# A layer of 16384 one-neuron experts, from gathered rows to one dense pass over the tables

## What is computed

```python
def block_fn(hb):                       # 128 tokens, width 1024
    t = hb.shape[0]
    q = (hb @ w_query).reshape(t, PEER_HEADS, 2, PEER_HALF)      # 8 heads, 2 halves of 128
    s = jnp.einsum('thpc,hpnc->thpn', q, sub_keys)               # 128 sub-keys a half
    v1, i1 = lax.top_k(s[:, :, 0], PEER_TOPK)                    # 16 each
    v2, i2 = lax.top_k(s[:, :, 1], PEER_TOPK)
    cand = (v1[..., :, None] + v2[..., None, :]).reshape(t, PEER_HEADS, PEER_TOPK * PEER_TOPK)
    cand_idx = (i1[..., :, None] * PEER_NKEYS + i2[..., None, :]).reshape(...)
    best, pos = lax.top_k(cand, PEER_TOPK)
    experts = jnp.take_along_axis(cand_idx, pos, axis=-1)        # of 16384
    gate = jax.nn.softmax(best, axis=-1)
    u = expert_u[experts]                                        # rows of 1024
    vsel = expert_v[experts]
    act = jax.nn.gelu(jnp.einsum('thkd,td->thk', u, hb), approximate=False)
    return jnp.einsum('thk,thkd->td', gate * act, vsel)
```

## Time and profile before

| | |
|---|---|
| timed runs | 1367.41, 1369.69 and 1555.32 us |
| median | 1369.69 us |
| profiled execution, first to last instruction (its own time) | 1367.2 us |
| PE / DVE / ACT / POOL busy | 1162.8 / 713.7 / 392.0 / 286.6 us |
| moved by DMA | 446.79 MB, 327 GB/s over the span |
| indirect DMA alone | 268.45 MB |
| first and last gather issued | 269.16 and 919.93 us |
| last matmul on gathered rows ends | 941.2 us |

### The profile page before, as it was taken

The page is one execution under the profiler, slowest core; times in us unless marked ns, Lnnn a source line. Parts: engine busy times, 40 slices in busy tenths (PEclk is TensorE's granted clock), DMA queues, the critical chain, the costliest instruction groups (busy, mean ns, idle before and its releaser), DMA issues.

```text
span 1367.2 us, 16345 instructions
## 1 busy us (share of the span) xinstructions
PE 1162.8 (85%) x5986; PEld 716.0 (52%) x5986; DVE 713.7 (52%) x1850; ACT 392.0 (29%) x1094; POOL 286.6 (21%) x275
## 2 busy tenths in 40 slices
PE   6999998989999987778777777778999998867896
PEld 4887877874555532223222223325978875332342
DVE  2365532487677777767777666644752515311112
ACT  2203532223333333333233334222531423000011
POOL 0000000024444444444444434440030000000000
PEclk9999999999999999999999999999999998999999
DMA  9711237399999999999999999997521474999996
GB/s 392 302 62 62 93 116 315 147 406 395 421 421 421 422 420 421 422 421 399 422 422 422 421 419 399 421 422 313 196 94 63 185 292 177 427 424 424 425 388 257
DMA packets 60283, 446.79 MB, mean 327 GB/s; under 512 B 6704, under 2 KB 7088, under 8 KB 10160
## 3 DMA queue, kind: packets, MB, share of 16 engines
q0 software_dynamic: 36864, 268.45, 47.5%
q1 hardware_dynamic: 22912, 175.97, 31.8%
q10 hardware_dynamic: 432, 1.40, 0.3%
HBM read 444.74 MB, written 1.05 MB: 326 GB/s over the span
## 4 chain that ended last, share of the span: by engine, by line
PE 52%; DMA 34%; DVE 6%; ACT 4%; issue 2%; SPq 0%; POOL 0%; DVEq 0%; ACTq 0%
DMA arena<-uv_in,arena 26%; PE bank L2478 12%; PE bank L2344 9%; DMA wring<-moe_in 4%; PE bank L2575 4%; PE bank L2821 3%; PE bank L2441 3%; PE bank L2837 2%; DMA wring<-stream_in 2%; DVE arena L1809 2%; PE bank L2780 2%; DMA arena<-moe_in 2%; PE bank L2572 2%; PE bank L2807 2%; PE bank L637 1%
## 5 line engine op out<-in xcount | busy, mean ns | idle before, releaser
L2478 PE MATMUL bank<-arena 128*128 128x512 f32 x1024 | 474.1, 606 | 116.9 <-ACT arena L1069 116.9
L1809 DVE CUSTOM_DVE_ANT_0 arena<-arena 128x1024 f32<-128x1024 f32 x256 | 314.0, 1226 | 192.5 <-DMA arena<-uv_in,arena 191.5
L787 POOL DMA_INDIRECT arena<-uv_in,arena x256 | 272.0, 1063 | 650.1 <-PE bank L2478 365.7
L2478 PEld LDWEIGHTS bank<-arena 128*128 128x128 f32 x1024 | 186.6, 191 | 374.3 <-ACT arena L1069 192.7
L1061 ACT ACTIVATE arena<-arena 128x2 f32<-128x2 f32 x128 | 26.2, 205 | 410.0 <-DVE arena L1809 409.8
L2344 PE MATMUL bank<-wring,arena 128*128 128x256 f32 x608 | 134.1, 381 | 1.0 <-DVE arena L1384 1.0
L2344 PEld LDWEIGHTS bank<-wring,arena 128*128 128x128 f32 x608 | 115.2, 191 | 17.7 <-DVE arena L1384 1.1
L1069 ACT ACTIVATE arena<-const,arena 128x128 f32<-128x128 f32 x256 | 86.7, 385 | 0.0
L2441 PEld LDWEIGHTS bank<-arena,wring 128*128 128x128 f32 x384 | 57.0, 196 | 20.2 <-issue 15.3
L2821 PE MATMUL bank<-arena 128*32 128x512 f32 x288 | 59.7, 616 | 7.5 <-DMA arena<-moe_in 4.9
L2821 PE MATMUL bank<-wring,arena 128*32 128x512 f32 x288 | 59.7, 620 | 7.2 <-DMA wring<-moe_in 7.2
(11 more groups left out here) (458 smaller groups left out, 1318.5 us busy)
## 6 DMA issues: line engine op xcount, KB each, us to landing
wring<-stream_in SPq DMA_DIRECT2D x67, 1024.0 KB, 8.9
wring<-moe_in SPq DMA_DIRECT2D x14, 2048.0 KB, 17.9
arena<-moe_in SPq DMA_DIRECT2D x26, 1024.0 KB, 17.7
arena<-moe_in SPq DMA_DIRECT2D x12, 2048.0 KB, 18.7
wring<-moe_in SPq DMA_DIRECT2D x13, 1024.0 KB, 14.2
arena<-uv_in,arena POOLq DMA_INDIRECT x256, 12.8
arena<-moe_in SPq DMA_DIRECT2D x4, 512.0 KB, 10.7
wring<-moe_in SPq DMA_DIRECT2D x4, 512.0 KB, 11.2
```

Of the source, the lines that this page charges most:

```text
L787: pool.indirect_dma_start(G[:, j, :], None, uv_d, src).then_inc(gathered[j], 16)
L1809: v.tensor_tensor_reduce(out=junk, in0=G[:, j, 0:D], in1=h2[:, t, :], scale=1.0, scalar=0.0, op0=ALU.mult, op1=ALU.add, accum_out=dots[:, ...
L2478: ins = mm(bank[1 + 2 * tile + c][:, :], diag[:, j, :], G[:, j, D + c * 512:D + (c + 1) * 512], start=False, stop=False, skip_group_check= ...
```

## The change

The gathers, dots and diagonals go. The whole layer is done for all 16384 experts and all 256 tokens:

- The ring and the arena become one tensor `big`, in which `G` is now 128 x 256 floats a partition: G[j, i, t] belongs to the expert i * 128 + j and token t. A block i is 128 experts with the same first key.
- **u pass** (PE L2575 in the changed kernel). SP brings u in pairs of blocks, `u_in(m)`: four transfers, each of 256 columns of the pair's 256 rows to 32 partitions. DVE transposes each block in squares of 32 (`turn_u`, L1737) into one of two buffers `UT`; PE multiplies with `h2P`, h2 with its features in the matching order (made by `spread_h2`), 8 matmuls of 256 tokens a block; ACT writes the GELU of a pair into G. Between the blocks DVE does the selection, 3 pieces a block up to block 35, then 2; PE the remaining 12 queries, one every third block; POOL the lookup of the chosen keys (seven instructions a unit), which was `decode` on DVE.
- **Weights** (PE L2586). The sum over a token's slots of gate times the two one-hot key vectors is a 128 x 128 matrix. For each token one matmul forms it: `hot2` is the one-hot of the second key (POOL subtracts, ACT takes Abs and then Relu of 1 - x), `hot1` the one-hot of the first times the gate (DVE, L1854). They go in 64 batches of four tokens. DVE multiplies G with them (`weigh`, L1861), in place.
- **v pass** (PE L2595). SP brings v in pairs of blocks, `v_in(c)`, five buffers, in which three stand where the raw u was; PE accumulates all eight groups of 128 features of all tokens in four banks. The last four pairs are done tile by tile. SP loads the second block's first eight chunks in between.
- Ahead of the layer `project_out(1)` comes before the first query, the modulation group 5 is loaded after the output projection's chunks instead of before, and the query chunks have places of their own.

```diff
+            def u_in(m):
+
+                i = block_of(2 * m)
+                for a in range(4):
+                    sp.dma_start(raw[m % 3][32 * a:32 * a + 32],
+                                 uv_d[i * P:(i + 2) * P, a * T:(a + 1) * T].rearrange("(g r) c -> r g c", r=32))\
+                      .then_inc(uv_here[RAW_HOME[m % 3]], 16)
+
+            def v_in(c):
+
+                sp.dma_start(vbuf[c % V_RING], uv_d[2 * c * P:(2 * c + 2) * P, D:].rearrange("(b j) d -> j b d", b=2))\
+                  .then_inc(uv_here[c % V_RING], 16)
...
+            sp.wait_ge(rms_sum, 4)
+            u_in(2)
+            for m in range(3, PAIRS_U):
+                sp.wait_ge(ut_ready, 2 * (m - 3) + 2)
+                u_in(m)
+            for c, last in ((1, 61), (4, 62), (0, 63)):
+                sp.wait_ge(ut_ready, 2 * last + 2)
+                v_in(c)
+            sp.wait_ge(uv_used, BLOCKS_U)
+            v_in(2)
+            v_in(3)
+            for c in range(V_RING, PAIRS_U):
+                sp.wait_ge(uv_used, BLOCKS_U + c + 1 - V_RING)
+                v_in(c)
...
         def _(pool):
-                pool.indirect_dma_start(G[:, j, :], None, uv_d, src).then_inc(gathered[j], 16)
...
+            for b in range(N_BATCH):
+                if b >= 4:
+                    pool.wait_ge(w_built, b - 3)
+                nc.gpsimd.tensor_tensor(hot2[b % 4], bc(lane, 1, BATCH), bc(key2T[:, BATCH * b:BATCH * (b + 1)], 2, P),
+                                        ALU.subtract).then_inc(hot2_ready, 1)
...
+                act.wait_ge(uv_used, 2 * m + 2)
+                nc.scalar.activation(G[:, i:i + 2, :].rearrange("p i t -> p (i t)"), bank[1 + m % 2][:, :], ACT.Gelu)\
+                  .then_inc(u_out, 1)
...
+            def turn_u(n):
+
+                m, b = n // 2, n % 2
+                dve.wait_ge(uv_here[RAW_HOME[m % 3]], u_landed(m))
+                if n >= 2:
+                    dve.wait_ge(uv_used, n - 1)
+                v.transpose(UT[b].rearrange("p c (g r) -> p g c r", g=4),
+                            raw[m % 3][:, 4 * b:4 * b + 4, :].rearrange("p g (c s) -> p g c s", c=8)).then_inc(ut_ready, 1)
...
+            pieces = selection()
+            for n in range(BLOCKS_U):
+                if n >= 2:
+                    turn_u(n)
+                advance(pieces, 3 if n < PIECES_FAST else 2)
+                if n in GATES_AT:
+                    gates_of(GATES_AT.index(n))
...
+                for q in range(BATCH):
+                    tok = slice(BATCH * b + q, BATCH * b + q + 1)
+                    ins = v.tensor_scalar(hot1[:, b % 2, q], lane, key1T[:, tok], gateT[:, tok], ALU.is_equal, ALU.mult)
+                ins.then_inc(hot1_ready, 1)
+
+            def weigh(b):
+
+                dve.wait_ge(w_built, b + 1)
+                some = G[:, :, BATCH * b:BATCH * (b + 1)]
+                v.tensor_tensor(some, some, bank[W_BANK[b % 4]][:, :].rearrange("p (t i) -> p i t", t=BATCH), ALU.mult)\
+                 .then_inc(bank_taken, 1)
+
+            keys_hot(0)
+            keys_hot(1)
+            dve.wait_ge(u_out, PAIRS_U)
+            for b in range(N_BATCH):
+                weigh(b)
+                if b + 2 < N_BATCH:
+                    keys_hot(b + 2)
...
-            def weighted_rows(first, slots=range(GS)):
...
+                pe.wait_ge(ut_ready, n + 1)
+                for c in range(KD):
+                    ins = mm(bank[1 + m % 2][:, b * T:(b + 1) * T], UT[b][:, c, :], h2P[:, c, :],
+                             start=c == 0, stop=c == KD - 1)
+                ins.then_inc(uv_used, 1)
...
+            pe.wait_ge(u_out, PAIRS_U)
+            for b in range(N_BATCH):
+                pe.wait_ge(hot1_ready, b + 1)
+                pe.wait_ge(hot2_done, b + 1)
+                if b >= 4:
+                    pe.wait_ge(bank_taken, b - 3)
+                for q in range(BATCH):
+                    ins = mm(bank[W_BANK[b % 4]][:, q * P:(q + 1) * P], hot2[b % 4][:, q], hot1[:, b % 2, q],
+                             start=True, stop=True)
+                ins.then_inc(w_built, 1)
...
+            pe.wait_ge(bank_taken, N_BATCH)
+            for c in range(PAIRS_U - V_TAIL):
+                pe.wait_ge(uv_here[c % V_RING], v_landed(c))
+                for b in range(2):
+                    ins = values(c, b, range(KD), slice(0, T))
+                ins.then_inc(uv_used, 1)
```

More of the change, by code:

```diff
@@ L55, with chunk_slot, chunk_turn @@
 WSLOTS = 8
+RING = WSLOTS * CHUNK
+EXTRA_SLOTS = {C_Q: 8, C_SK: 9}
+def chunk_slot(n):
+    if C_Q <= n < C_IN2:
+        return EXTRA_SLOTS[n] if n in EXTRA_SLOTS else n - C_SK - 1
+    return n % WSLOTS
+def chunk_turn(n):
+    return sum(chunk_slot(m) == chunk_slot(n) for m in range(n + 1))
 SM = {}
@@ L81 @@
 CN_FIRST = CN["eps"].stop
-ARENA = 28928
+ARENA = 29400
 PER = 4
@@ new lines, in _ @@
+            for b in range(N_BATCH + 1):
+                if b < N_BATCH:
+                    act.wait_ge(hot2_ready, b + 1)
+                    steps[0] += 1
+                    nc.scalar.activation(hot2[b % 4], hot2[b % 4], ACT.Abs).then_inc(act_step, 1)
+                if b > 0:
+                    act.wait_ge(act_step, steps[0] - (b < N_BATCH))
+                    nc.scalar.activation(hot2[(b - 1) % 4], hot2[(b - 1) % 4], ACT.Relu, bias=ones[:, 0:1], scale=-1.0)\
+                      .then_inc(hot2_done, 1)
@@ new lines, in advance @@
+            def advance(pieces, n):
+                for _ in itertools.islice(pieces, n):
+                    pass
+            add_mixed(0)
+            finish_all(normed(0))
+            add_mixed(1)
+            turn_u(0)
+            turn_u(1)
+            finish_all(normed(1))
+            modulation(5)
+            pieces = selection()
[5 more added lines that the diff above has]
+                    gates_of(GATES_AT.index(n))
```

732 lines of the change are left out of this document (340 added, 392 removed).

## The result

The changed kernel takes 1800.57 us (median of four runs, 1797.19 to 1802.0), against 1369.69 us for the kernel before (median of 1367.41, 1369.69 and 1370.96): a ratio of 1.315, with a 95% interval of 1.3128 to 1.3177. It is slower by 31.5%. One run of before at 1555.32 us belongs to a slower state of the chip and is left out. The profiled execution took 1802.0 us, its span 1800.2.

A forecast was written before the change was run, and what follows sets the result against it. DMA's u stream at 210 GB/s was to bound most of the u pass: u's end at 600, weights 107, v 226.5 and what follows 423.5 gave a 1357 us span, median 1359, range 1318 to 1402.

The forecast's parts named there:

- The step that failed: u pass on PE: 8 matmuls of 128x256 a block at 0.216 us, 1.73 us a block, 221 us in all.
- 3.84 us for two: Before the u pass: price of two queries on PE, so four early queries were put at 8 us.
- The bound named for u: u pass: DMA's u stream at 210 GB/s, 2.49 us a block, above DVE's 2.2 and PE's 1.73.
- the three candidates: u pass: PE at 1.73 us a block, DVE at 2.7 then 2.2, DMA between 1.25 and 5.
- The stream at half the rate: u pass: four transfers to 32 partitions each move 210 GB/s, 4.97 us a pair of blocks.
- stream hidden: Rival for the u pass: four transfers together fill all DMA engines; 1328 us, chance 0.28 (hidden or nearly).
- The weights: Stage between u and v: 64 batches at 1.65 us with DVE the longest, 107 us.
- for some 30%: Weights: PE's busy share; its lower clock hidden there (0.5 us becomes 1), 3 us added at v's start.
- strided product: Rival for the weights: DVE's product on G takes double, 44 us more, 1403; weights dearer had 0.12.
- what follows the layer: After the v pass: 2.5 us off the 426.0 us of before, 423.5.
- the slow stream at 1659: u stream's lower end, a quarter of the rate: u pass 610 us, kernel 1659; at most 2 in 100.
- the prediction's own sign of error: u pass: the prediction called itself wrong if this pass is longer than 340 us.

The follow-up runs named there:

- the third experiment: Changed kernel with POOL making the differences of only the first four weights batches, ACT reusing those buffers for the other 60: 1761.28 us.
- the last: Kernel with u turned in HBM and one-instruction matmuls, with ACT making hot2 alone and POOL's subtraction gone: 1249.77 us, 0.9125 against before.

## Why the prediction was wrong

**The step that failed** is "a block is 8 matmuls of 128x256, and 272 of that form ran in 58.71 us, 0.216 each, so 1.73 us a block and 221 us in all", and with it the v pass, "960 matmuls of 128x256 at 0.216". The 0.216 is right. But the rows of the trace count instructions, the 8 and the 960 were counted in the code, and a float32 matmul of the code is two instructions. What stood ahead of the prediction shows it already: the order of the code lists a projection (L2414) with 64 matmuls and a query (L2441) with 16, and the earlier trace rows show the same two as x128 and x32. A group of before says it too. The code makes two matmuls of 512 columns for each of 256 pairs, 512:

```profile
L2478 PE MATMUL bank<-arena 128*128 128x512 f32 x1024 | 474.1, 606 | 116.9 <-ACT arena L1069 116.9
```

With 3.46 us a block, u is 128 x 3.46 + 12 queries with scores x 4.0 = 491, the 491.2 measured; v is (960 x 0.216 + 128 x 0.113) x 2 = 443.6, against 444.8. Both corrections, 181 and 218, are 399 of the 443 us by which the span was missed. The same error is in the queries ("3.84 us for two" is one query of 16 matmuls) and in the weights' four matmuls, which are eight instructions. The two projections, carried over as whole rows of 14.46 us, did not have it. That the u pass still began within 5 us of the forecast is partly luck: the four early queries took 15 us, not 8, and the projections ended at 265, not 259.5; against that the two spreadings took 4 us, not 7, and 290 held 8.5 us more than the terms listed for it.

The Trainium skill, "FP8 and Floating Point Precision", section "TensorE Precision Notes", says that true FP32 takes four passes through the array. The runs agree: 3.8 times between the two forms, in two instructions. The rule was not weighed in the prediction; it would not have changed the sum by itself, since 0.216 us for 256 columns holds two of the passes, and looks like one slow matmul as long as the counts are not compared.

**The bound named for u** was the wrong one of the three candidates, and rightly described. The stream at half the rate, taken as 210 GB/s, is 218 to 223 wherever it is the limit. Here the Trainium skill's figure for 32 partitions in "SBUF — State Buffer", section "Door 1: The DMA port swizzle", 218, was closer. Its statement in the section "Can I just issue two DMAs to hit both halves?" that transfers side by side hardly help each other also agrees. Neither is proved here, since no run moved pieces of 1 KB to 128 partitions. In the changed kernel the stream is hidden: 152 GB/s are wanted. So the rival "stream hidden" has its outcome but not its mechanism: four transfers together moved 219 GB/s where PE was out of the way, not 421, and PE was slow enough to hide even half the rate. Its time, 1328, had the same error of PE's count.

**The weights** were forecast at 107 us and took 147. The rhythm, 1.65 us a batch with DVE the bound, is what DVE does when POOL is away (1.64, in 104.9 us). DVE's loss beside POOL, 29 us, was put at nothing without a reason. The lower clock was weighed and called hidden, with PE busy "for some 30%"; but with eight instructions a batch PE was busy for 68% at a granted clock of 0.75, and DVE waited for it 17.3 us, where it waited 8.8 with POOL away and the clock at 1.00. The rival "strided product" was wrong: L1861 takes 680 ns, the 689 of an ordinary one. POOL took 1.05 us a batch, not 1.37; its harm was not its length but that it ran beside DVE.

**The other terms.** Transposition 1.245 us (forecast 1.2); beginning of u, 294.6 (290); what follows the layer, 422.2 (423.5). No rival reached beyond 1404 except the slow stream at 1659, which was for another reason. The missing rival was "PE's passes cost twice", and the prediction's own sign of error, a u pass longer than 340 us, is how it showed.

**Where the expected gain went.** Streaming each table once did save the transfer: the chain has no DMA in the layer. The bound moved to PE, whose two passes hold 2048 float32 matmuls of 256 columns or their equal, 885 us at 0.432 each; gathering took some 670 for all of it. With one instruction a matmul the time is the kernel before's within 2% (1363.17 against 1366.84). With the u table laid out anew and turned in the input, and POOL out of the weights, the transfers hold most of both passes and the gain appears: 1249.77 against 1368.05, at the price of the lower mantissa bits.

## What to carry to other kernels

Before a duration from a row is multiplied by a number from the code, find one line in the trace whose count can be worked out from the code, and compare: a float32 matmul counts twice. A dense form that replaces a gather trades bytes for columns on PE; price the columns at the datatype's rate first (here 0.43 us for 128x256 in float32, 0.114 in bfloat16), since a saving in transfers doesn't show while PE is the longer. Where one engine holds the first part of a pass and the transfers the rest, add the parts; the larger of the two totals is too low. And an engine that is off the critical path may still slow the one that is on it: POOL's instruction of 1 us cost DVE up to 0.8 us a batch.

## What the runs showed of the hardware

- DVE's tensor_scalar of 128 elements took 0.275 us each in a row of four, and 0.475 on average when a POOL tensor_tensor fell among the four; the product with one operand in PSUM, 0.68 us, showed no such loss in the mean (680 with POOL, 686 without).
- Four transfers to 32 partitions each in pieces of 1 KB, queued back to back, moved 218 to 223 GB/s in all from 400 to 575 us of the two runs that waited for them. Single ones to 128 partitions in pieces of 4 or 8 KB moved 333 to 402 late in the same pass with three buffers of 1 MB, and 403 to 412 in v with five. Whether partitions or pieces make the difference was not separated.
- PE's granted clock was 0.75 (a mixture of 2.4 and 1.2 GHz) with PE busy for 68% of a window of the weights, and 1.00 (2.4 GHz) with 71% in the third experiment and 64% (31.77 of 50 us) in the last. Why it fell in the one and not in the others stays open.
- A view with a stride of two over float32 data fed PE at 0.114 us for 256 columns, with the array's clock at 1.00; the same operands as bfloat16 without the stride were not tried.
- DVE turns 128x1024 floats in blocks of 32 in 1.23 to 1.245 us, about as long as its dot of as many takes (1226 ns).
